# DVE takes each low half of the weight split one attention job later in its order, in the woven stages of blocks two and three

## The reference

```python
# block two
proj = rms_norm_2(x, norm_pre) @ w_in          # q, k, v, gates z, merge gates
o_a = nsa_attention(q_a, kc, vc, ks, vs, kw, vw, gates_a, slopes)    # 8 heads x 3 branches
o_b = moba_attention(q_b, k_b, v_b, slopes)                         # 8 heads
m = sigmoid(gate_a) * (o_a * silu(z_a) @ w_a) + sigmoid(gate_b) * (o_b * silu(z_b) @ w_b)
x = x + rms_norm_2(m @ w_o, norm_post)
# block three, each of two layers
proj = rms_norm_3(x) @ w_in[l]
mix = concatenate([o_a, o_b, o_c, o_d])        # neighbourhood, differential, dilated, latent attention
x = x + mix @ w_o[l]
x = x + (silu(h @ w_gate[l]) * (h @ w_up[l])) @ w_down[l]
```

## Time and profile before

| | us |
|---|---|
| median of 3 runs (2399.67 to 2404.65) | 2403.23 |
| the profiled execution's own time | 2403.64 |
| its span, first to last instruction | 2401.8 |
| TensorE busy in the span | 1834.0 (76%) |
| DVE busy | 831.7 (35%) |
| ACT busy | 631.2 (26%) |
| mean granted clock of TensorE | 0.87 of full speed |

### The profile page before, as it was taken

The page is one execution under the profiler, slowest core; times in us unless marked ns, Lnnn a source line. Parts: engine busy times, 40 slices in busy tenths (PEclk is TensorE's granted clock), DMA queues, the critical chain, the costliest instruction groups (busy, mean ns, idle before and its releaser), DMA issues.

```text
span 2401.8 us, 33822 instructions
## 1 busy us (share of the span) xinstructions
PE 1834.0 (76%) x13686; PEld 1341.0 (56%) x13686; DVE 831.7 (35%) x1687; ACT 631.2 (26%) x1107; POOL 58.9 (2%) x94
## 2 busy tenths in 40 slices
PE   6999766556655555565548888879879997888998
PEld 4789621111111111111118878778779977778996
DVE  2364510000000000000015355744555544555553
ACT  1334310000000000000012454425523432543332
POOL 2000000000000000000000001000100000000000
PEclk8999887887788788878878899979979997988999
DMA  9786489999999999999993332152155543043540
GB/s 348 281 284 242 176 353 418 418 418 418 418 418 418 417 418 418 418 418 418 417 401 135 141 106 83 42 197 71 60 169 164 188 145 106 36 140 115 176 177 34
DMA packets 193908, 613.55 MB, mean 255 GB/s; under 512 B 8772, under 2 KB 62082, under 8 KB 161024
## 3 DMA queue, kind: packets, MB, share of 16 engines
q1 hardware_dynamic: 189856, 604.46, 65.4%
q0 software_dynamic: 3200, 7.14, 1.0%
q10 hardware_dynamic: 736, 0.38, 0.1%
HBM read 610.85 MB, written 5.03 MB: 256 GB/s over the span
## 4 chain that ended last, share of the span: by engine, by line
PE 46%; DMA 36%; DVE 5%; ACT 4%; issue 4%; DVEq 4%; SPq 0%; POOL 0%; ACTq 0%; POOLq 0%
PE psum L1246 45%; DMA ring<-in_w_down_e 18%; DMA ring<-in_w_up_e 17%; ACT ring_r L636 2%; DVEq L2007 2%; DMA ring<-in_w_in 1%; DVE ring_r L645 1%; DMA x<-in_x 1%; DVEq L2022 1%; PE psum L1326 1%; DVEq L1729 1%; PE psum L1550 1%; ACT arena L1109 1%; DVE stat L2008 1%; ACT arena L950 0%
## 5 line engine op out<-in xcount | busy, mean ns | idle before, releaser
L1246 PE MATMUL psum<-ring,arena 128*32 128x512 f32 (+1 forms) x4316 | 544.0, 648 | 323.6 <-DMA ring<-in_w_up_e 139.4
L1246 PE MATMUL psum<-xR,ring_r 128*128 128x256 f32 x4416 | 578.3, 291 | 10.0 <-DVE xR L1713 7.0
L1246 PEld LDWEIGHTS psum<-xR,ring_r 128*128 128x128 f32 x4416 | 553.7, 197 | 22.3 <-issue 11.9
L1246 PEld LDWEIGHTS psum<-ring,arena 128*32 128x32 f32 x4316 | 155.2, 135 | 677.4 <-issue 221.0
L645 DVE TENSOR_TENSOR ring_r<-ring,ring_r 128x1024 fp32r<-128x1024 f32 (+2 forms) x332 | 377.2, 1172 | 345.0 <-ACT ring_r L636 344.9
L636 ACT CAST ring_r<-ring 128x1024 fp32r<-128x1024 f32 (+2 forms) x332 | 319.5, 1004 | 509.7 <-PE psum L1246 486.1
L1246 PE MATMUL psum<-arena 128*128 128x64 f32 (+8 forms) x1346 | 216.1, 367 | 67.2 <-DVE arena L2028 21.5
L1246 PE MATMUL psum<-ring_r,xR 128*128 128x256 f32 (+3 forms) x1488 | 213.0, 303 | 13.2 <-DVE xR L1713 11.0
L1246 PEld LDWEIGHTS psum<-ring_r,xR 128*128 128x128 f32 x1488 | 201.5, 213 | 18.5 <-DVE xR L1713 10.7
L1246 PEld LDWEIGHTS psum<-arena 128*128 128x128 f32 (+5 forms) x1346 | 145.9, 188 | 110.0 <-issue 58.0
L1931 DVE TENSOR_TENSOR arena<-arena,psum 128x512 f32<-128x512 f32 x16 | 11.0, 688 | 495.2 <-PE psum L1246 495.2
(11 more groups left out here) (199 smaller groups left out, 980.8 us busy)
## 6 DMA issues: line engine op xcount, KB each, us to landing
ring<-in_w_up_e SPq DMA_DIRECT2D x64, 2048.0 KB, 25.6
ring<-in_w_gate_e SPq DMA_DIRECT2D x64, 2048.0 KB, 23.7
ring<-in_w_down_e SPq DMA_DIRECT2D x64, 2048.0 KB, 27.1
ring<-in_w_in SPq DMA_DIRECT2D x30, 2048.0 KB, 11.8
ring<-in_w_ada SPq DMA_DIRECT2D x12, 2048.0 KB, 9.7
ring<-in_w_gate SPq DMA_DIRECT2D x22, 1024.0 KB, 5.4
ring<-in_w_up SPq DMA_DIRECT2D x22, 1024.0 KB, 8.1
ring<-in_w_down SPq DMA_DIRECT2D x10, 2048.0 KB, 7.9
```

The lines of the kernel that those rows point to most:

```text
L1246: return nc.tensor.matmul(o, l, r, start=s, stop=e)
```

## The change

Only the program of DVE changes, and in it only the place of `low.half` for the splits of the woven lists. A split entry of the list is kept in `behind`. After the next job's `least` and `finish` (and what belongs to that job) one entry is taken from it and done. In block two this holds for all 30 splits. In block three it holds for those from the first part of `qb0` on (14 in each layer, the pair behind job 34 among them, which is now done behind jobs 35 and 36); the four pairs ahead of that stay. Where a second split follows with only a part and no job between, both wait in the list and are done behind one job each. ACT's and TensorE's programs are the same.

```diff
+WOVEN3 = PLAN3.index(("part", "qb0", 0, 8))
...
+            behind = []
             for kind, n, *_ in PLAN2:
                 if kind == "job":
                     least(n, job2(n), j_s, j_t, j_min)
...
                         v.tensor_tensor(oA, oA, zA, ALU.mult).then_inc(y_done, 1)
+                    if behind:
+                        low.half(*behind.pop(0))
                 elif kind == "split":
-                    low.half(*n)
+                    behind.append(n)
+            while behind:
+                low.half(*behind.pop(0))
...
-                for kind, n, *_ in PLAN3:
+                behind = []
+                for at, (kind, n, *_) in enumerate(PLAN3):
...
                             head_norms(l)
+                        if behind:
+                            low.half(*behind.pop(0))
                         continue
                     if kind == "split":
-                        low.half(*n)
+                        if at < WOVEN3:
+                            low.half(*n)
+                        else:
+                            behind.append(n)
                         continue
...
+                while behind:
+                    low.half(*behind.pop(0))
                 for j in range(NJ3 - 3, NJ3):
```

## The result

The changed kernel takes **2337.46 us** (median of 5 runs, 2333.75 to 2343.54) against 2403.23 before (5 runs, 2399.67 to 2404.65): a ratio of **0.9735, 95% interval 0.9718 to 0.9753**, or 65.8 us less. The profiled execution took 2340.59 us, its span is 2338.8, so 63.0 shorter than before.

What follows compares the result with a forecast made beforehand. Bound: TensorE's waits in three woven stages, behind a ring of ACT cast, DVE low half, DVE minimum, ACT exponential. Terms 20.0 + 20.4 + 2.0 + 5.6 = 48.0 us off 2403.6 gave 2355.6 us; range 2344 to 2380.

Steps and rivals of the forecast that it cites:

- The low half behind the job's work costs nothing: Block three: DVE needs 6.0 of 8.7 us per four jobs, and TensorE's parts cover the later low half.
- Block two's waits, 20.0 us: Block two's woven stage: of 22.1 us of TensorE waits 20.0 go, 2.1 stay for ACT alone; bounds 10 and 22.1.
- The woven layers' waits, 20.4: Block three's woven stretches: of 11.2 us of waits a layer 10.2 go, 20.4 for two; bounds 10 and 22.4.
- the tail, 2.0 us: End of each block three layer, pair behind job 34 moved: 1.0 us a layer, 2.0 in all; bounds 0 and 7.9.
- The clock, 5.6 us: Low-clock stretches behind longer waits go: 1.6 us in block two, 1.3 and 0.7 a layer; bounds 0 and 7.0.
- the prediction's own signs of being wrong: Block two's named waits still over 10 us, waits for line 645 at piece heads, or clock sinking where it was 1.00.
- clock not won: Rival, all stages: waits go but low-clock stretches of the same total fall elsewhere; 42.4 us won, 2361 us; chance 0.18.
- a layer's unheld steps (73 us of 85): Block three layer: job steps without waits sum to 73 us where the window has 85, so 12 us to win.
- All of it: Rival, all stages and tails: every upper bound is won, 59.4 us, giving 2344 us; chance 0.10.
- ACT as the ring: Rival, woven stages: ACT's own work keeps half of the waits; 24 us won, 2380 us; chance 0.16.
- Slower through DVE's next job: Rival, woven stages: the moved low half blocks DVE's next job, 71 us lost against 48 won, 2427 us; chance 0.03.
- No effect: Rival, woven stages: each wait is really due to ACT's cast ahead of probabilities, 2400 to 2404 us; chance 0.03.

Runs made afterwards that it cites:

- the double low half: Changed kernel with DVE making each woven low half twice, first into a scratch tile, except a layer's first and last pair: 2370.73 us, 0.9873.

## Why the prediction was right or wrong

**What bounds the kernel, and the place of the effect: right.** The difference of the spans lies in the three stages, and each block alone gave its part.

**The low half behind the job's work costs nothing: right, and nearly at its limit.** My count (6.0 of 8.7 us of DVE in a layer) held. For block two I had made no such count, and there the double low half shows how little room is left.

**Block two's waits, 20.0 us:** measured 21.6. The 2.1 us that I left to ACT alone were mostly not its own; 0.4 us was left for ACT's copy.

**The woven layers' waits, 20.4, and the tail, 2.0 us:** measured 12.3 + 11.6 = 23.9, against 22.4. The kb0 wait stayed as said (1.0 us), and so did the other 1.0 us one. The first layer's woven stretch went from 85.0 to 69.8 us, where I had said 72. The waits were good to 1.5 us each; together 45.5 against 42.4.

**The clock, 5.6 us:** measured 9.1, with another split. Block two gave 0.4 and not 1.6, because a low stretch of 0.67 appeared at its start, where the clock had been at 1.00 before. That was one of the prediction's own signs of being wrong, and the only one that fired; by the run of block three alone it isn't the change's doing. The layers gave 8.7 and not 4.0. I took the first layer's windows for both, though the second had two low windows in a row behind its first job (0.54, 0.61), not one; I counted half of the stretch behind the kb0 piece because its wait stays, but it went whole; and I left out the tails, which gave about 1.3 of it. The rule that I set against this term, from the Trainium skill, "TensorE: Matmul & The Clock Gate", section "What's actually happening", that the gate's decisions come on a schedule of its own, has the start of block two for it. It also has two stages of kernels in which the order is that of before: the first layer with the change in block two alone, where no low stretch follows the first job and the kb0 piece, and block two with the change in block three alone, where none follows at 1441 us. So the rival "clock not won" holds for block two; in the layers 8.7 us were won between these two executions, of which some may be the execution's and not the order's. How much stays open; in that first layer 4.7 us went with no change of the order. So how far this term came out above the forecast may in part be chance.

**What was missing: the lost overlap, 8.3 us.** This is the step that failed, and the largest part of the miss: "What TensorE should win is its waits" took the idle time on record as the whole price of a wait. It is 0.2 us more for each. Against the forecast's 48.0 us the profiled execution gave 62.9, so 14.9 more: 3.1 by the waits, 3.5 by the clock and 8.3 by a term that the sum didn't have.

The rows to see it were there: I counted a layer's unheld steps (73 us of 85), but never set a step with a wait beside the same step without one. And the count, which should have shown it, was itself too long. It has jobs 0 to 34 whole, but the window of the earlier trace rows opens behind the part and the scores of job 0 (1649.91 and 1651.42) and closes behind job 34's first matmuls. The stretch took 69.8 us in the changed kernel, so 15.2 are won there and not 12; of the 14.0 us of idle time and clock 1.0 stays, so 13.0. The two counts agreed by luck: an error of 3 us in the one hid the 2 us of lost overlap that the other lacked.

**The bounds.** "All of it" came to 59.4 us because it summed idle time and clock alone. By the terms as measured the profiled execution lies 62.9 us lower and the medians 65.8; the last 2.9 us between the two are within what executions of one kernel differ by (2333.75 to 2343.54), and no profile explains them.

**The rivals.** ACT as the ring: refuted; the waits for its copy fell from 10.4 to 0.4 us in block two with ACT's program unchanged, and with the cast moved as well the time is the same. Slower through DVE's next job: refuted at this size; at twice it the low halves do hold TensorE, though that kernel too is 30.6 us faster than before. No effect: refuted.

## What to carry to other kernels

Work that isn't urgent but stands in an engine's order ahead of a step of a latency loop is paid for by the whole loop; put it behind *all* steps of that engine that the loop needs, not only the first, and count what room is left there. Price the waits that go away by comparing whole steps, held and unheld, and not by idle time: here the idle time was 45.5 of 62.9 us. Check that a count of steps and the window that it is held against begin and end at the same instruction. Where waits of one to three us vanish, the low clock behind them may vanish with them; read its price in every repetition of the stage and in more than one execution.

## What the hardware showed that I had not expected

- A wait of TensorE ahead of the values matmuls cost some 0.23 us on top of its idle time, whatever its length (from 0.09 to 1.68 us): in the step shown, 0.16 us of overlap with the transpose ahead of it and 0.07 us in the group itself. Where the values' operand is 15 rows high it cost only 0.02 to 0.06.
- Two executions of different kernels repeat most unheld steps of TensorE to 0.01 or 0.02 us, so job-by-job differences between two traces can be trusted to that size.
- The same waits in the same order (the first layer of before and of the kernel with block two alone, up to the kb0 piece: 3.1, 1.1, 1.0 and 1.6 us) were followed by low clock in one execution (0.67 and 0.66 in the earlier trace rows, behind the first job and behind kb0) and not in the other (1.00 in both places). Block two's low stretch at 1441 us came and went in the same way.
